# Two-block transformer kernel: the last head pairs' outputs by token halves, delta rows asked for by POOL, norms overlapped

## The reference, cut to what matters

```python
def chunk_gated_delta_rule(q, k, v, g, beta):          # chunks of 64 tokens, g = log a
    cum = jnp.cumsum(g, axis=-1)
    decay = jnp.exp(jnp.where(causal, cum[..., :, None] - cum[..., None, :], -jnp.inf))
    k_beta = k * beta[..., None]
    a = jnp.where(strict, jnp.einsum('bhnid,bhnjd->bhnij', k_beta, k) * decay, 0.0)
    rhs = jnp.concatenate([v * beta[..., None], k_beta * jnp.exp(cum)[..., None]], axis=-1)
    sol = lax.linalg.triangular_solve(a + eye, rhs, left_side=True, lower=True, unit_diagonal=True)
    attn = jnp.einsum('bhnid,bhnjd->bhnij', q, k) * decay
    ...
    def step(state, xs):
        v_new = u_c - jnp.einsum('bhck,bhkv->bhcv', w_c, state)
        o = jnp.einsum('bhck,bhkv->bhcv', q_c, state) + jnp.einsum('bhij,bhjv->bhiv', attn_c, v_new)
        state = state * last_c[..., None, None] + jnp.einsum('bhck,bhcv->bhkv', k_c, v_new)
        return state, o

def gated_deltanet(h, w_in, w_conv, a_log, dt_bias, w_norm, w_out):
    ...
    qkv = causal_conv_silu(qkv, w_conv)
    ...
    o = rms_norm(o, w_norm) * jax.nn.silu(z.reshape(b, t, GDN_V_HEADS, GDN_HEAD_DIM).astype(jnp.float32))
    return o.reshape(b, t, GDN_V_DIM).astype(h.dtype) @ w_out

def second_block(...):
    h = jnp.concatenate([meta, x], axis=1)              # 16 + 512 tokens, 1024 features
    for layer in range(2):
        hn = rms_norm(h, attn_norm[layer])
        mix = gated_deltanet(hn, ...) if layer == 0 else mlstm(hn, ...)
        h = h + mix
        h = h + squared_relu_mlp(rms_norm(h, ffn_norm[layer]), ff_up[layer], ff_down[layer])
    return h[:, 16:]
```

## Time and profile before

| | us |
|---|---|
| median of 3 runs | 4182.79 |
| lowest, highest | 4182.3, 4184.68 |
| the profiled execution | 4180.28 |
| its span | 4178.5 |
| PE busy | 3740.6 (90%) |
| PEld busy | 3464.9 (83%) |
| DVE busy | 2611.2 (62%) |
| ACT busy | 1534.5 (37%) |
| POOL busy | 744.0 (18%) |

### The profile page before, as it was taken

One profiled execution on the slowest core, in us unless ns is written; L12 is line 12 of the kernel. 1 busy time (PEld: TensorE's weight loads), 2 busy tenths in 40 slices (PEclk: granted clock), 3 DMA queues, 4 the chain that ended last, 5 costly groups with the idle time before them and its releaser, 6 DMA issues.

```text
span 4178.5 us, 60676 instructions
## 1 busy us (share of the span) xinstructions
PE 3740.6 (90%) x24575; PEld 3464.9 (83%) x24575; DVE 2611.2 (62%) x5087; ACT 1534.5 (37%) x2722; POOL 744.0 (18%) x589
## 2 busy tenths in 40 slices
PE   7999989989978999998868898888789999978999
PEld 5667769879978999898668887777689998978999
DVE  4664337989977999999456666666452433555342
ACT  4555223335543333333433333332341424444231
POOL 0000004546732333332111011111000001110000
PEclk9999999989989999999889999999899999998999
DMA  3112224448879999998121112211122221112221
GB/s 112 56 61 71 86 66 132 142 138 265 277 221 330 322 336 332 334 332 286 32 63 54 53 46 56 58 50 36 45 83 90 87 62 51 61 41 76 91 92 66
DMA packets 232342, 542.33 MB, mean 130 GB/s; under 512 B 18664, under 2 KB 120552, under 8 KB 232064
## 3 DMA queue, kind: packets, MB, share of 16 engines
q1 hardware_dynamic: 128592, 355.38, 26.1%
q0 software_dynamic: 37440, 136.33, 9.4%
q10 hardware_dynamic: 66032, 46.75, 3.6%
HBM read 492.14 MB, written 46.25 MB: 129 GB/s over the span
## 4 chain that ended last, share of the span: by engine, by line
PE 61%; DVE 25%; ACT 6%; issue 4%; DMA 2%; POOL 0%; SPq 0%; DVEq 0%; ACTq 0%; POOLq 0%
PE bank L95 61%; DVE wl L122 5%; DVE acc L132 3%; DVE H L122 2%; DVE row L168 2%; ACT wh L116 2%; DMA qe<-scratch 1%; DVE yc L132 1%; DVE eq L122 1%; DVE aal L122 1%; PE bank L98 1%; DVE fs L122 1%; DVE sq L132 1%; ACT Xh L116 1%; DVE Xl L122 1%
## 5 line engine op out<-in xcount | busy, mean ns | idle before, releaser
L95 PE MATMUL bank<-Xh,wh 128*128 128x272 f32 (+3 forms) x3680 | 1235.5, 336 | 60.9 <-ACT ft L116 25.7
L95 PE MATMUL bank<-Xl,wh 128*128 128x272 f32 (+3 forms) x3680 | 1168.9, 318 | 0.0
L95 PE MATMUL bank<-Xh,wl 128*128 128x272 f32 (+3 forms) x3680 | 1167.5, 317 | 0.0
L122 DVE TENSOR_TENSOR wl<-raw,wh 128x1024 fp32r<-128x1024 f32 (+1 forms) x536 | 576.4, 1094 | 459.2 <-ACT wh L116 458.3
L116 ACT ACTIVATE wh<-raw 128x1024 fp32r<-128x1024 f32 (+1 forms) x632 | 589.1, 953 | 695.2 <-PE bank L95 652.4
L95 PEld LDWEIGHTS bank<-Xh,wh 128*128 128x128 f32 x3680 | 715.3, 194 | 128.3 <-issue 59.6
L95 PEld LDWEIGHTS bank<-Xh,wl 128*128 128x128 f32 x3680 | 713.4, 194 | 20.9
L95 PEld LDWEIGHTS bank<-Xl,wh 128*128 128x128 f32 x3680 | 716.2, 195 | 17.2 <-issue 0.2
L122 DVE TENSOR_TENSOR H<-H,bank 128x384 f32<-128x384 f32 (+3 forms) x522 | 250.7, 490 | 329.7 <-PE bank L95 326.7
L95 PE MATMUL bank<-aah,wh 128*128 128x384 f32 x1024 | 355.5, 347 | 43.1 <-DVE wl L122 23.3
L122 POOL TENSOR_TENSOR wl<-raw,wh 128x1024 fp32r<-128x1024 f32 x96 | 277.6, 2894 | 509.9 <-ACT wh L116 509.5
(11 more groups left out here) (300 smaller groups left out, 6090.0 us busy)
## 6 DMA issues: line engine op xcount, KB each, us to landing
raw<-in_u SPq DMA_DIRECT2D x128, 512.0 KB
raw<-in_v SPq DMA_DIRECT2D x128, 512.0 KB
raw<-in_up SPq DMA_DIRECT2D x64, 512.0 KB, 4.2
raw<-in_down SPq DMA_DIRECT2D x64, 512.0 KB, 4.1
scratch<-gb ACTq DMA_DIRECT2D x12, 2048.0 KB, 13.7
gj<-scratch SPq DMA_DIRECT2D x32, 768.0 KB
raw<-in_w_gdn SPq DMA_DIRECT2D x48, 512.0 KB
raw<-in_w_att SPq DMA_DIRECT2D x36, 512.0 KB
```

Source lines behind the costliest of these rows:

```text
L95: return Issued(self, self.q and self.q.matmul(out, l, r, start=start, stop=stop), 1)
L122: return Issued(self, self.q and self.q.tensor_tensor(out, a, b, op), 1)
```

## The change

Five things change; all are in the second block.

1. **Norm.** DVE's subtraction of block k is written behind the multiplication of block k+1.
2. **Delta rows.** `rows_in` and `beta_in` become programs of POOL (they are gone from SP) with semaphores of their own (row0 to row3). Pair 0's rows are asked for behind the gates as before, pair 1's behind the pair steps of pair 0. The gates' steps yield less in between, so that they come earlier in step 0.
3. **Start of a pair.** decay(p, 2) stands behind pair(p, 0) and pair(p, 1); the taps of the convolution are spread over four steps; RO has three buffers, and out_gdn squares group 2 at the end of the scan and finds all three inverse roots first; the weight of out_gdn in the merge goes from 10 to 8.
4. **Last pair, before its outputs.** Of GDN pair 7 and mLSTM pair 3, groups 0 and 1 get their norm, gate and split inside the scan (at c=6 and c=7), group 2 behind it. Their buffers lie elsewhere (ZG.place, OX.place), so that pair 7 doesn't wait for pair 6's output.
5. **Last outputs.** The last output projection is done by `last_outputs`: first all blocks of half 0, then of half 1. The mean squares of half 0 end at block 1 of half 1, and the norm of half 0 is written between blocks 3 to 6 of half 1. Three up slabs are prepared early (`prepare(1)`), `more_room` gives three more split buffers (two before) in memory of the scan, and `ffn` has no fence; it does the norm of half 1 only.

The loops lose their last turn (range(11) to range(10), range(6) to range(5)). mLSTM gets the same edits as GDN in 4 and 5; of these the diff shows the end.

```diff
         def ffn(layer):
-            sums_end(f"ffn{layer}", HALVES)
-            f = fence()
+            sums_end(f"ffn{layer}", HALVES[1:])
             top[0] = base
-            xf = normed(f"ffn{layer}", HALVES)
+            xf = normed(f"ffn{layer}", HALVES, done=(0,))
             FH, FL = FFH[layer], FFL[layer] = alloc2("f", 16, 528)
             FT = FTR[layer] = Ring([alloc("ft", 272) for _ in range(8)])
-            more_room((f"up{layer}", f"down{layer}"), 1, 2, f)
+            assert top[0] <= ROOM[layer][0]
+            top[0] = ROOM[layer][1]
             if layer == 0:
...
+        def last_outputs(layer, names, xs, signal, ring):
+            ws = [slab(*n) for n in names]
+            key = f"ffn{layer}"
+            oh, ol = xs
+            sums_begin(key, HALVES, PA)
+            behind = []
+            for hf, (a, b) in enumerate(HALVES):
+                for fb in range(8):
+                    g = group(PD, [(w, fb) for w in ws],
+                              lambda e, a=a, b=b: (oh[:, e, a:b], ol[:, e, a:b]), b - a,
+                              lambda e, hf=hf: ((signal, names[0][1] // 2, e, hf),))
+                    dense_now(g)
+                    do("resid", g, fb, a, b)
+                    given_back(g, "resid", g)
+                    behind.append((a, fb, "resid", g))
+                    if len(behind) > 2:
+                        sums_part(key, *behind.pop(0))
+                    if hf and fb == 1:
+                        sums_end(key, HALVES[:1])
+                    if hf and fb > 2:
+                        for k in ((fb - 3) * 2, (fb - 3) * 2 + 1):
+                            if k < 8:
+                                norm_block(key, *HALVES[0], k, ring=ring)
+                    if not hf and fb % 2 or hf and fb == 0:
+                        prepare(1)
+            for x in behind:
...
-        RO = Ring([alloc("ro", 384) for _ in range(2)])
...
+        gdn_end = top[0]
+        top[0] = bb_at
+        OX.place(7, alloc2("og", 2, 528), ("xmm", 7, 5, 2))
+        assert top[0] <= work
...
+        XQ7 = Ring(YC.bufs, given=(("qk", 7, 0, 1), ("qk", 7, 1, 1), ("vd", 7, 2, 1), ("vd", 7, 3, 1)))
...
                     yield 1
             do("gdn_softplus")
-            yield 2
+            yield 1
...
             do("rows_out")
-            yield 4
+            yield 2
...
-                yield 2
+                yield 1
             do("gdn_exp")
-            for p in range(2):
-                for g in range(3):
-                    rows_in(p, g)
+            for g in range(3):
+                rows_in(0, g)
             beta_in(0)
             beta_in(1)
-            yield 1
+            yield 10
 
         def dense_gdn(t):
 
...
+                        if n < 4 and not hf:
+                            XC.take((p, n))
                         do("gdn_take", p, n, hf)
                         given_back(g, "gdn_in", p, n, hf)
                         if hf and n < 4:
-                            after(1, lambda p=p, n=n: convolve(p, n))
+                            for tap in range(4):
+                                after(4 - tap, lambda p=p, n=n, tap=tap: convolve(p, n, tap))
                             if n < 2:
...
             do("keys_twice", p)
-            for g in range(3):
+            for g in range(2):
                 do("decay", p, g)
             yield 1
             for g in range(3):
+                if g == 2:
+                    do("decay", p, 2)
                 for n in ("kk", "vt"):
                     PA.take((n, p, g))
                 do("pair", p, g)
...
                 beta_in(3 * p + g + 2)
                 yield 1
             QS.give(p, ("kk", p, 2), ("qe", p, 2))
+            if p == 0:
+                for g in range(3):
+                    rows_in(1, g)
             for g in range(3):
                 PA.take(("ke", p, g))
...
             sums_now(("out", p, 1))
-            yield 1
             inverse(0)
             inverse(1)
             yield 2
+            sums_now(("out", p, 2))
+            inverse(2)
+            yield 1
             gate(0)
-            out_squares(p, 2)
             yield 1
             gate(1)
-            sums_now(("out", p, 2))
             yield 1
-            inverse(2)
-            yield 2
             gate(2)
             yield 1
...
                 if c in (3, 6):
                     out_squares(p, c // 3 - 1)
+                if p == 7 and c == 6:
+                    sums_now(("out", 7, 0))
+                    sums_now(("out", 7, 1))
+                    for g in range(2):
+                        do("rms_inv", ("out", 7, g))
+                        do("times_z", ("out", 7, g))
+                if p == 7 and c == 7:
+                    for g in range(2):
+                        do("gdn_gate", 7, g)
+                    for e in range(2):
+                        do("gdn_split", 7, e, 0)
+            out_squares(p, 2)
...
             if t > 1:
-                streams.append((scans(t), 10 * (t > 2) + 26 * (t < 10)))
+                streams.append((scans(t), 8 * (t > 2) + 26 * (t < 10)))
             merge(*streams)
+        sums_now(("out", 7, 2))
+        do("rms_inv", ("out", 7, 2))
+        do("times_z", ("out", 7, 2))
+        do("gdn_gate", 7, 2)
+        for e in range(2):
+            do("gdn_split", 7, e, 1)
+        room_at = gdn_end - 7 * 1152
+        ROOM[0] = room_at, more_room(("up0", "down0"), 1, 3, (("so", 7, 8), ("vnm", 7, 8), ("sn", 7, 7, 1)), room_at)
+        last_outputs(0, [("gdn_out", 14), ("gdn_out", 15)], OX.at[7], "ogl", XQ7)
...
+        ROOM[1] = room_at, more_room(("up1", "down1"), 1, 3, (("mo", 3, 8), ("msn", 3, 7), ("mnum", 3, 2)), room_at)
+        last_outputs(1, [("ml_out", 6), ("ml_out", 7)], OX1.at[3], "mogl", XQ3)
...
+                q = clear(dv, ring, ("q",) + key + (k,))[:, 0:b - a]
                 dv.stt(q, H[:, k, a:b], col(key[0], k), r, ALU.mult, ALU.mult).then_inc("xq", *key, k)
-                dv.wait_ge("xh", *key, k)
-                dv.tt(XL[:, k, a:b], q, XH[:, k, a:b].bitcast(F32), ALU.subtract).then_inc("xl", *key, k)
+                for j in [k - 1] * (k > 0) + [7] * (k == 7):
+                    dv.wait_ge("xh", *key, j)
+                    dv.tt(XL[:, j, a:b], ring.at[("q",) + key + (j,)][:, 0:b - a], XH[:, j, a:b].bitcast(F32),
+                          ALU.subtract).then_inc("xl", *key, j)
...
                 for n in range(4):
                     po.wait_ge(f"spill{n}", 4 * AHEAD - 4 + n)
+
+            def rows_in(p, g):
+                m = 3 * p + g
+                name = f"rows{m % 2}"
+                if p < 2:
+                    po.wait_ge("dup", 3, 1)
+                    po.wait_ge("nbe", 0)
+                    po.wait_ge("rows_out", 2)
+                else:
+                    po.wait_ge("so", p - 2, 3 * g + 2)
+                if m > 1:
+                    po.wait_ge(name, (m - 2) // 3, (m - 2) % 3, 1)
+                for i, x in enumerate((DD.at[p], QE.at[p])):
+                    po.dma(three(x, g), scratch3[i, 3 * g:3 * g + 3, 2 * p:2 * p + 2, :].rearrange(
+                        "c h i -> c (h i)").partition_broadcast(128)).then_inc(name, p, g, i)
+
+            def beta_in(p, g):
+                b = clear(po, SQ, ("beta", p, g))[:, 0:384]
+                po.wait_ge("rows_out", 2)
+                po.dma(b.rearrange("p (c x) -> p c x", c=3), scratch3[2, 3 * g:3 * g + 3, 2 * p:2 * p + 2, :].rearrange(
+                    "c h i -> c (h i)").partition_broadcast(128)).then_inc(f"beta{SQ.slot['beta', p, g]}", p, g)
 
...
```

202 lines of the change are left out of this document (110 added, 92 removed).

## The result

| | before | after |
|---|---|---|
| median | 4183.53 | 4082.37 |
| lowest, highest of 4 runs | 4182.3, 4184.68 | 4076.89, 4084.21 |
| profiled execution (its span) | 4180.28 (4178.5) | 4081.27 (4079.4) |
| mean granted clock | 0.948 | 0.957 |

What follows compares the result with a forecast made beforehand. The prediction took PE to bound the second block, with its gaps and the low clock behind them to be won. A to F (-20 - 8 - 42 - 6 - 21 - 12) gave -109, 4071.3, and with the median's 2.5, 4074; range 4052 to 4118.

Steps and rivals of the forecast that it cites:

- A: First pair of GDN: earlier beta and third-group reads shorten PE's 23.95 us wait; -20 us, range -14 to -27.
- D: Start of GDN's last pair: PE's 6.10 us wait for pair 6's third-group norm goes; -6 us, range 0 to -8.
- E: GDN into feed-forward 0: second up set starts earlier, gaps shrink; -21 us, range -10 to -28.
- C: Starts of pairs 2 to 7: POOL's earlier reads cut PE's 9.3 us gap to 2.3; 7 us each, -42 us.
- F: mLSTM into feed-forward 1: same edit as at GDN's end, second up set starts earlier; -12 us, range -4 to -17.
- B: Norms: block 0.9 us instead of 1.35; 5 at GDN, 4 at mLSTM, first block costs 1; -8, range 0 to -14.
- Rivals 1 and 2: POOL's row reads dear in pair loop: 2.3 us per issue, 4112 (chance 0.14); from 4.2, slower than before (0.04).
- The rule on POOL's DMAs: Pair loop: POOL issues beside DVE two-port copies up to five times 0.76, 3.8 us; most of C would be gone.
- Rival 4: Pair starts: gap filled, but DVE keeps the start, half the gain goes into ro,ones and conv; C -20, 4096; chance 0.12.
- Rival 3: Layer ends give back less, as the norm inside the scan delays last chunks; E -8, F -5, 4094; chance 0.13.

Runs made afterwards that it cites:

- a4_norm: Changed kernel with each norm subtraction ahead of the next multiplication again, in all norms: 4114.73 us, ratio 0.9835.
- a1_sp: Changed kernel with the reads of delta rows and beta back on SP's queue, with the old semaphores: 4062.51 us, ratio 0.9715.
- b3_pool: Kernel before the change with only its reads of delta rows and beta moved to POOL's queue: 4162.74 us, ratio 0.9948.
- a2_decay: Changed kernel with decay of group 2 ahead of the products of groups 0 and 1 again, reads still on POOL: 4081.17 us, ratio 0.9759.
- a11_sp_decay: Changed kernel with reads back on SP's queue and decay of group 2 in front again: 4085.16 us, ratio 0.9764.
- a10_taps: Changed kernel with the four taps of each convolution in one step again: 4100.27 us, ratio 0.9801.
- a6_behind: Changed kernel with norm, gate and split of the last pair's groups 0 and 1 behind the scan, both layers: 4081.08 us, ratio 0.9757.
- a78_slabs_fence: Changed kernel without early preparation of the three up slabs and with the fence before the feed-forward, both layers: 4095.46 us, ratio 0.9794.
- a9_out: Changed kernel with out_gdn's old order and weight 10 for pairs 0 to 6, three RO buffers kept: 4084.77 us, ratio 0.9765.
- b9_gates: Against a1_sp: gates and split of the pair before moved into the scan behind chunks 0 and 1: 4058.59 us, ratio 0.9703.

## Why the prediction was right, and where it was not

**The sum.** -109 was predicted against the profiled execution, -99.1 came. The 10 us are: A and GDN's norm 6, D and E 2.5, the first block 1.8, C 0.8, less 1.2 that mLSTM's norm and F brought more. The first block's 2.8 arise well ahead of GDN's norm, and kernels with the same first block differ by as much.

**A** and GDN's norm were to bring 25; 19.0 came by pair 1. With 6.8 of them the norm's (a4_norm), A itself brought some 12, less than the 14 at the low end of its range. PE's waits between the norm and pair 1, before (2031 to 2190 us), then after (2033 to 2175):

```profile
PE bank L98 <- DVE dd L122: 23.9, 1, 23.9
PE bank L98 <- ACT vd L116: 7.1, 2, 4.2
...
PE bank L98 <- ACT vd L116: 12.2, 2, 7.1
PE bank L95 <- ACT rt L116: 6.0, 1, 6.0
```

The long wait behind the beta read went whole, where the prediction left 4 us of it. But the convolutions' results came late instead: the waits for vd grew by 5.1 us, that for rt,ones, 3.5 before, by 2.5. The first group of pair 0 now starts behind 7.13 us of that wait for vd, 6.6 us later than before. The prediction put such delays at nothing. The queue has no part in it (a1_sp, b3_pool).

**B** was right where it was argued: 6.8 and 4.4 by a4_norm against 5 and 4. The first block's two norms showed no cost. What the prediction didn't see is that the overlap carries E and F: with it undone, 21 of their some 37 us are lost.

**C** had its size (7 predicted, 114.1 - 107.3 = 6.8 came), and that was largely luck. What the prediction read of the gap held: with POOL asking, the rows are there when DVE's decays begin, and the gap of 9.7 falls to 3.8 alone (b3_pool) and 3.2 in after, where 2.3 was said. The step that failed is the next one, "7 us each, 42 in all": it counts a gap closed on PE as time won. The queue alone takes 5.0 to 5.5 us per pair from the waits of cst,vd, and 2.1 (b3_pool) or 1.6 (a2_decay against a11_sp_decay) from the step; most of the rest PE waits elsewhere. With the reads left on SP, decay 2 behind gives 109.1 - 104.9 = 4.2 and the rest of the change the other 5.0 of 9.2. Of those 5.0, 3.7 are idle time of PE, which the prediction left as it was. In before (2184 to 2859 us) PE waited 12.7 us for ro,ones, 12.0 for rc, 8.0 for tb and 7.1 for st; in a11_sp_decay it is nothing, 1.0, nothing and 2.1, against 14.9 for the new rt,ones. The taps are the likely larger part (3.1 in a10_taps, tried with POOL asking). On top of that order POOL asking costs 2.4. Of the parts undone one at a time, the one that the prediction built on is the only one without which the kernel is clearly faster. Two errors hid each other: the taps got nothing in the sum, and the queue got the whole gap.

**D and E** came to -24.5 against -27. Inside E the parts were mis-sized: the groups inside the scan bring nothing (a6_behind), early slabs and no fence bring 13 over both ends (a78_slabs_fence), the norm's overlap 21. The delay that the prediction put at 4.4 us is as large as the gain. **D** is inside the -24.5 and was not tried alone (a9_out comes nearest): the long wait for ro,ones ahead of the last scan is gone, but PE now waits 7.8 us for ta at 2814.91, where before shows no such wait. **F** held (-12.4 against -12). The clock rose as said, to 0.957.

**The rivals.** Rivals 1 and 2 fell with the issue times of after, 0.76 us where they need 2.3 and over 4.2. The rule on POOL's DMAs that the prediction weighed showed no effect: the longest of the 72 issues took 0.895 us. (The prediction's "the others have two sources" overlooks DVE's transposes ta<-tb, which have one; the 11 issues that ran beside them took 0.81 us at most.) Rival 4 is what happened to the queue's gain: as cst,vd lost 35 us, rt,ones took up 22.0 and ta 10.7, behind DVE's work at the start of a pair. Rival 3 was not seen at the ends as a whole, though its mechanism is (a6_behind).

**Not settled.** What carries the 2.4 us by which POOL asking costs: DVE's slowed instructions, the late beta reads, or the issues themselves. The third RO buffer was never undone. b9_gates was not tried with less work on DVE, and which part of the gates or of pair 1's rows shortens pair 0's start wasn't taken apart. Each profile is one execution.

## What to carry to other kernels

When a change does two things against one wait, price each alone and then both: here the order of DVE's work was enough, and the change of queue on top cost 20 us. Work given to a lightly used engine is not free for that: look at what stands behind it there and at what runs beside it. And a gap on the busiest engine that is closed by moving another engine's work is worth only what that engine doesn't ask back at the next wait: look for the wait that is late next, before and after. Last, compare like with like: a whole time can hide 10 us of the part that was changed behind 6 us of chance in a part that wasn't.
